# Attention units of a hybrid decoder layer: both heads' scores before both heads' transposes on TensorE

## The reference, cut to what matters

```
s = einsum('bhqd,bhkd->bhqk', q, k) * dh ** -0.5
s = where(k_pos <= q_pos, s, NEG_INF)
p = softmax(s, axis=-1)
o = einsum('bhqk,bhkd->bhqd', p, v)
...
y = concatenate([head_norm(y_moba), head_norm(y_ml) * sigmoid(lo), head_norm(y_nsa)])
x = x + rms_norm(y @ w_out)
x = x + rms_norm(square(relu(rms_norm(x) @ w1)) @ w2)
```

## Time and the profile before

| | |
|---|---|
| runs | 636.16 us median of 3 (635.68 to 637.22) |
| the profiled execution | 636.81 us, its span 635.0 us |
| mean granted TensorE clock | 0.99 of full speed |
| PE busy | 606.6 us (96% of the span) |
| DVE, ACT, POOL busy | 386.8, 302.1, 247.4 us |
| the 24 attention units | from 183.05 us to about 241 us of the span |

### The profile page before, as it was taken

How to read it: one execution, slowest core, us unless ns; L and a number is a source line. 1 busy time by engine, 2 the same in 40 slices (tenths; PEclk the granted TensorE clock), 3 DMA queues, 4 the chain that set the end, 5 groups by cost and what they waited for, 6 DMA issues and landing times.

```text
span 635.0 us, 8412 instructions
## 1 busy us (share of the span) xinstructions
PE 606.6 (96%) x3172; PEld 499.2 (79%) x3172; DVE 386.8 (61%) x665; ACT 302.1 (48%) x541; POOL 247.4 (39%) x120
## 2 busy tenths in 40 slices
PE   2999999999989989999999999999999999999995
PEld 2988888886876667889987888888888888888884
DVE  4526031104878877288499968569577595681656
ACT  5415264107566974255563564425545445453422
POOL 4422527402526351005336564172533723812611
PEclk9999999999989989999999999999999999999999
DMA  9442449513240222002704353250340613203002
GB/s 281 136 132 68 132 117 233 127 40 116 85 133 10 59 82 85 1 1 67 266 1 165 101 170 96 76 190 2 133 133 2 211 55 132 67 1 126 40 34 100
DMA packets 45724, 63.50 MB, mean 100 GB/s; under 512 B 6616, under 2 KB 34292, under 8 KB 45684
## 3 DMA queue, kind: packets, MB, share of 16 engines
q1 hardware_dynamic: 45524, 62.71, 32.0%
q10 hardware_dynamic: 160, 0.26, 0.2%
HBM read 58.51 MB, written 2.10 MB: 95 GB/s over the span
## 4 chain that ended last, share of the span: by engine, by line
PE 89%; DVE 5%; ACT 2%; issue 1%; DMA 1%; POOL 1%; SPq 0%; DVEq 0%; ACTq 0%
PE ps L1616 20%; PE ps L1617 19%; PE ps L1618 19%; PE ps L2006 7%; PE ps L2008 7%; PE ps L2007 7%; PE ps L1878 2%; PE ps L1758 1%; PE ps L1863 1%; DMA raw<-in_w_in 1%; PE ps L1782 1%; PE ps L1783 1%; DVE stat L1290 1%; DVE probsT L1302 1%; PE ps L1934 1%
## 5 line engine op out<-in xcount | busy, mean ns | idle before, releaser
L1618 PE MATMUL ps<-xT_h,ring_l 128*128 128x512 f32 (+1 forms) x384 | 143.1, 373 | 0.0
L1616 PE MATMUL ps<-xT_h,ring_h 128*128 128x512 f32 (+1 forms) x384 | 143.0, 372 | 0.0
L1617 PE MATMUL ps<-xT_l,ring_h 128*128 128x512 f32 (+1 forms) x384 | 143.0, 372 | 0.0
L661 POOL TENSOR_TENSOR ring_l<-raw_d,ring_h 128x1024 fp32r<-128x1024 f32 x25 | 67.4, 2707 | 130.8 <-ACT ring_h L931 130.8
L661 POOL TENSOR_TENSOR ring_l<-raw,ring_h 128x1024 fp32r<-128x1024 f32 x31 | 76.8, 2502 | 83.9 <-DVE xres L1459 44.4
L604 POOL TENSOR_TENSOR ring_l<-raw,ring_h 128x2048 fp32r<-128x2048 f32 (+1 forms) x16 | 69.5, 4353 | 85.6 <-ACT ring_h L679 85.6
L1553 DVE TENSOR_TENSOR y<-ps,y 128x512 f32<-128x512 f32 x90 | 61.2, 688 | 52.6 <-PE ps L2008 52.2
L1616 PEld LDWEIGHTS ps<-xT_h,ring_h 128*128 128x128 f32 x384 | 72.6, 189 | 12.9
L1617 PEld LDWEIGHTS ps<-xT_l,ring_h 128*128 128x128 f32 x384 | 72.3, 188 | 12.6
L1618 PEld LDWEIGHTS ps<-xT_h,ring_l 128*128 128x128 f32 x384 | 72.3, 188 | 12.6
L2006 PE MATMUL ps<-ring_h,a_h 128*128 128x512 f32 x196 | 77.4, 395 | 0.0
(11 more groups left out here) (248 smaller groups left out, 995.5 us busy)
## 6 DMA issues: line engine op xcount, KB each, us to landing
raw<-in_w_mlp SPq DMA_DIRECT2D x16, 1024.0 KB, 5.4
raw_d<-in_w_mlp SPq DMA_DIRECT2D x16, 1024.0 KB, 6.0
raw<-in_w_in SPq DMA_DIRECT2D x9, 1024.0 KB, 5.3
raw<-in_nsa_cmp_w SPq DMA_DIRECT2D x8, 512.0 KB, 7.2
xres<-in_x SPq DMA_DIRECT2D x4, 512.0 KB, 5.9
raw<-in_w_out SPq DMA_DIRECT2D x2, 1024.0 KB, 6.4
raw<-in_w_out SPq DMA_DIRECT2D x4, 512.0 KB, 4.3
out<-xres SPq DMA_DIRECT2D x8, 256.0 KB, 2.1
```

The costliest lines, as they stand in the source:

```text
L661: nc.gpsimd.tensor_tensor(slot(ring_l, n), slot_source(n), slot(ring_h, n).bitcast(F32), ALU.subtract).then_inc(lo_done, 1)
L1616: nc.tensor.matmul(o, sh, mh, start=start, stop=False)
L1617: nc.tensor.matmul(o, sh, ml, start=False, stop=False)
L1618: return nc.tensor.matmul(o, sl, mh, start=False, stop=stop)
```

## The change

On PE alone, the scores of both heads of a unit come first, then back or V, then the transposes of both heads. No instruction is added or removed; no other engine's program is touched.

```
 for u in range(NU):
     g, i = divmod(u, NT)
-    for m in range(2):
-        s = 2 * u + m
-        if s + 4 < 2 * NU:
-            score(s + 4)
-        if m == 0 and g and i == 3:
-            back(g - 1)
-        if m == 0 and g and i == 1:
-            values(g - 1)
+    for s in (2 * u + 4, 2 * u + 5):
+        if s < 2 * NU:
+            score(s)
+    if g and i == 3:
+        back(g - 1)
+    if g and i == 1:
+        values(g - 1)
+    for s in (2 * u, 2 * u + 1):
         transposes(s)
         if s == CT_S:
             cmp_transposes()
         if s in CO_S:
             cmp_out(CO_S.index(s))
-        if u == NU - 2 and m == 1:
-            pe.wait_ge(ml_y, 2)
-            y_transposes(0)
-            y_transposes(1)
+    if u == NU - 2:
+        pe.wait_ge(ml_y, 2)
+        y_transposes(0)
+        y_transposes(1)
```

## The result

| | before | changed | |
|---|---|---|---|
| time, median of 5 | 635.99 us (635.63 to 637.22) | 639.43 us (639.13 to 639.99) | ratio 1.0061, 95% interval 1.0049 to 1.0073 |
| profiled execution | 636.81 us, span 635.0 | 639.13 us, span 637.4 | +2.3 us |
| its mean granted clock | 0.990 | 0.994 | |

The changed kernel is slower by 0.6%, some 3.4 to 3.9 us; 638.5 was forecast. Two differences have to be told apart from the start: the two profiled executions lie 2.3 us apart (their spans 2.4), as forecast, and the medians 3.4.

A forecast was written before the change was run, and what follows sets the result against it. PE's order was taken as the kernel's, with the units a loop over PE, ACT and DVE. Shifts followed V by V left 2.4 us at the last V, rounded to +2.3: 636.16 + 2.3 = 638.5 us, range 635.9 to 640.2.

The forecast's parts named there:

- V waits for E(2u): V units: the second score, now ahead of V, waits for ACT's exp; V shifts 1.65 us in unit 9.
- T(2u) one score later: All units: the first head's transposes, and DVE and ACT work queued behind them, come 0.36 to 0.62 us later.
- two scores in a row: PE's stream in the units: adjacent scores cost up to 0.05 us a unit, 23 times, 0 to 1.15 us.
- The reading by weight loads alone: PE's stream: a weight load costs its columns over 1.2 in either order, so adjacent scores add 0.
- Unit 17 isn't carried on: V in unit 17 shifts 4.15 us, mostly absorbed where DVE stood behind POOL's subtraction; T(38) shifts 2.1.
- The compressed branch's 0.4 us: T(4) moves behind S(9), so gating, second cmp_out, mLSTM norm and POOL's products end about 0.4 us later.
- From the profile to the median: Whole kernel: the shift worked out on one profiled execution is added to the median, 636.16 + 2.3 us.
- the clock stays up: Rival, units 20 and 21: S(43) fills a wait, avoiding half rate; 1.5 us come back, 634.3 us, chance 0.11.
- Drowning: Rival: POOL's and DVE's queues set PE's waits, leaving 0.62 us at the last V; 636.8 us, chance 0.37.
- More half-rate stretches: Rival: new PE waits in units 17 and 21 bring clock 0.50, up to 1.7 us more; 640.2, chance 0.12.

The follow-up runs named there:

- e2: The kernel before with both scores first only in the five units with V: 639.01 us, ratio 1.0061.
- e4: The changed kernel, but in the V units V goes ahead of the second score: 636.51 us, ratio 1.0013.
- e3: The kernel before with both scores first in all units but the five with V: 635.58 us, ratio 1.0006.
- e1: The kernel before, unchanged, run again to see its own spread: 635.32 us, ratio 1.0004.
- e10: The kernel before with both scores first only in unit 17: ratio 0.9998, median +0.1 us.
- e11: The kernel before with both scores first only in unit 21: ratio 1.0029, median +1.7 us.
- e5: The changed kernel with all of ACT's extra work (MoBA splits, weight copies) one unit later: 643.50 us, ratio 1.0128.
- e6: The kernel before with all of ACT's extra work (MoBA splits, weight copies) one unit later: 641.76 us, ratio 1.0097.
- e9: The kernel before with both scores first only in unit 9: ratio 1.0035, median +2.2 us.

## Why the prediction was right, and where it was off

*V waits for E(2u).* Right, in all three places. In the changed profile V started at 204.05, 214.26, 224.70, 235.18 and 243.66 us; the working gave 204.2, 214.3 (2.2 late), 224.75, 235.2 and 243.7 (2.4 late). The waits ahead of the second score are 1.45, 1.26 and 1.27 us. e2 and e4 show that this step and the later T(2u) in the V units are the loss.

*T(2u) one score later.* Right, and right that it has slack elsewhere: the 19 other units cost nothing that can be told (e3), in the V units it is about 1.1 us (e4). The term for two scores in a row was sized right: two scores of 256 and six transposes take 1.28 us by turns in e1 (222.87 to 224.15) and 1.33 in pairs in e3 (223.99 to 225.32), so 0.05 a unit. The reading by weight loads alone, which made it 0, was not borne out. The sum of the term is bounded by e3, which has it in 17 of the 22 units with two scores (I had counted 23): +0.3 us by the medians, up to +1.0 by its interval.

*Unit 17 isn't carried on.* Right: e10 costs nothing. I had written that POOL's end and T(34) both come later together; in the changed kernel the step that used to stand behind POOL took 0.17 us.

*The compressed branch's 0.4 us.* POOL's L645 ends at 202.15, 0.2 later than before in a kernel whose units began 0.23 us earlier (182.82 against 183.05): 0.4. Little of it is carried on: in e2, where T(4) keeps its place, V in unit 9 comes 20.79 us behind the first score instead of 21.23, but the last V 60.68 instead of 60.84.

*From the profile to the median.* This is the step that failed: "the difference is carried to the median". The times of V, from the first score of unit 0, show where:

| V in unit | forecast shift | changed less the profile of before | changed less e1 |
|---|---|---|---|
| 9 | 1.65 | 1.72 | 1.73 |
| 13 | 2.2 | 2.43 | 2.44 |
| 17 | 4.15 | 4.33 | 4.35 |
| 21 | 2.4 | 2.60 | 4.17 |
| last | 2.4 | 2.57 | 3.79 |

Up to unit 17 both columns agree. In unit 21 the forecast took 2.4 from a V at 232.81 that stood behind a half-rate stretch, and by e1 few executions have that stretch. Beside e1, T(38) is 2.3 us late (47.53 and 45.26), as worked out, and V in unit 21 4.2. So unit 21 costs 1.5 us more by the last V (3.8 less 2.3), where the prediction had 0.3 (2.4 less 2.1); alone it cost 1.7 (e11). The changed kernel's own time for this V was met, because there V waits for the weight copy and E(42) and not for PE's stream. I had seen the stretch, and used it only for a rival (the clock stays up, faster). The clock did stay up, but before it mostly stayed up too; the other condition of that rival, E(42) out of the way, was not met either.

*The number.* +3.4 to +3.9 us lies above the forecast's own range of 1.9 to 3.2. That 638.5 came within 0.9 us of 639.43 is partly luck: the starting median of three, 636.16, lay 0.6 to 0.9 us above those of 11 to 29 executions (635.3 to 635.6) and made up for part of the loss that was missed.

*The rivals.* Drowning is refuted as a whole by the ratio, though it describes unit 17. More half-rate stretches did not come in the units of the changed kernel's profile; two of its five executions, with a mean clock of 0.992, took 0.5 to 0.9 us longer than the three with 0.994. They did come in e5 and e6, with waits of 3.6 us.

## What to carry to other kernels

When an instruction is moved ahead of a long one, list what it waits for: the wait moves with it, and the long instruction now stands behind it. Equal waits are not equal costs: follow each to the next place where another engine would have stopped the queue anyway. And before a change is summed against one profiled execution, compare that execution's granted clock and span with those of other executions of the same kernel; a stretch at half rate in the base can hide as much of a loss as it took. The same holds for a version: e9's stretch looked like a part of unit 9's cost.

## What was not expected of the hardware

A DVE instruction of 8 elements a row, two inputs in SBUF, took 0.17 us, 2.25, 3.97 or 4.51 us, depending on how much of POOL's subtraction of 128x2048 (4.5 us) was still to come when it started; started 0.05 us behind POOL's, it took POOL's whole length. The Trainium skill ("SBUF — State Buffer", section "SBUF: two separate sides") calls the port pair that the two engines share an exclusive lock, which the instruction that starts first holds to its end. By that rule the step can't end before POOL's, and the traces agree to 0.02 us (223.59 + 4.54 and 223.64 + 4.51 in e6, 226.45 + 4.55 and 227.05 + 3.97 in e5).

The same wait of PE, 1.93 us ahead of T(38), was followed by 3.4 us at clock 0.50 in the profile of before and by full clock in that of e1, with PE busy 1.49 of 3.42 us and 1.47 of 3.40 ahead of it. The wait of 1.95 us at the same place was followed by clock 0.50 in e9 and by 1.00 in e11 (227.90 to 231.30). So whether such a wait costs its own length or up to 1.5 us more differs from one execution to the next; what decides it was not shown.
